# More outputs of the mixing stage in the seven-product form, in another order of units

## The reference, cut to what matters

```python
def conformer_conv(a, conv_w, conv_b, norm_g, norm_b, w_o):
    gl = a[..., :CONV_WIDTH] * jax.nn.sigmoid(a[..., CONV_WIDTH:])
    y = conv_general_dilated(gl, ...31 taps, one filter per channel...) + conv_b
    y = jax.nn.silu(layer_norm(y, norm_g, norm_b))        # over the 1024 channels
    return y @ w_o

def mixer_merge(p, attn, w_attn_o, ..., w_gmlp_o, ..., w_conv_o, w_out):
    a_out = attn @ w_attn_o
    gu = jax.nn.gelu(p[..., GU_OFF:GV_OFF])
    gv = rms_norm(jax.nn.gelu(p[..., GV_OFF:CG_OFF]), gmlp_norm_g)
    g_out = chunk_spatial_gate(gu, gv, gmlp_ws, gmlp_bs) @ w_gmlp_o
    c_out = conformer_conv(p[..., CG_OFF:GATE_OFF], ...)
    gates = jax.nn.sigmoid(p[..., GATE_OFF:])              # three gates of 1024
    return (ga * a_out + gg * g_out + gc * c_out) @ w_out

for l in range(2):                                         # first block, D = 1024
    h = modulate(rms_norm(x, mix_pre_g[l]), sh1, sc1)      # 512 tokens
    p = h @ w_in[l]                                        # 7680 columns
    ...                                                    # the 256 context tokens alike in layer 0
    y = mixer_merge(...)
    x = x + g1 * rms_norm(y, mix_post_g[l])
    x = x + g2 * rms_norm(sq_relu_mlp(h2, w_ff1[l], w_ff2[l]), ffn_post_g[l])
...                                                        # then a second block, not touched
```

## Time and profile before

| | us |
|---|---|
| median of 3 runs | 3997.34 (3994.84 to 3998.64) |
| the profiled execution's own time | 3993.82 |
| its span | 3992.0 |
| PE busy | 3832.3 (96%) |
| DVE busy | 2353.9 (59%) |
| ACT busy | 945.8 (24%) |
| POOL busy | 290.2 (7%) |

### The profile page before, as it was taken

One profiled execution on the slowest core, in us unless ns is written; L12 is line 12 of the kernel. 1 busy time (PEld: TensorE's weight loads), 2 busy tenths in 40 slices (PEclk: granted clock), 3 DMA queues, 4 the chain that ended last, 5 costly groups with the idle time before them and its releaser, 6 DMA issues.

```text
span 3992.0 us, 34044 instructions
## 1 busy us (share of the span) xinstructions
PE 3832.3 (96%) x13274; PEld 2253.6 (56%) x13274; DVE 2353.9 (59%) x3855; ACT 945.8 (24%) x1917; POOL 290.2 (7%) x257
## 2 busy tenths in 40 slices
PE   7999989999999999999999999999999999899999
PEld 3454455555554554554445776646665458657665
DVE  5893548887405456556315599615666456745666
ACT  2103421111403111113125111312111334431111
POOL 1111000122021000000000012210000000000000
PEclk9999999999999999999999999999999999999999
DMA  7652001111212111111210122222222203011221
GB/s 272 213 200 76 6 22 63 43 64 42 95 61 59 63 63 43 63 63 54 75 64 6 44 84 85 85 79 100 85 85 85 81 33 87 9 42 64 85 96 72
DMA packets 126640, 300.51 MB, mean 75 GB/s; under 512 B 5394, under 2 KB 13634, under 8 KB 126480
## 3 DMA queue, kind: packets, MB, share of 16 engines
q1 hardware_dynamic: 108720, 239.73, 16.8%
q0 software_dynamic: 17760, 58.61, 4.4%
HBM read 296.14 MB, written 2.18 MB: 75 GB/s over the span
## 4 chain that ended last, share of the span: by engine, by line
PE 86%; DVE 9%; ACT 2%; DMA 2%; issue 1%; POOL 0%; DVEq 0%; SPq 0%; ACTq 0%
PE psum L447 32%; PE psum L2494 15%; PE psum L2366 14%; PE psum L2418 12%; PE psum L2360 3%; PE psum L1127 2%; PE psum L2463 2%; PE psum L2446 1%; DVE sb_kvt L2797 1%; DMA sb_rc<-in_ada_w 1%; DVE sb_rc L2797 1%; PE psum L1233 1%; DMA sb_ra<-in_ada_w 1%; ACT sb_rb L2047 1%; ACT sb_rc L2047 1%
## 5 line engine op out<-in xcount | busy, mean ns | idle before, releaser
L447 PE MATMUL psum<-sb_ring,sb_rc 128*128 128x512 f32 x868 | 393.3, 594 | 7.5 <-DVE sb_rc L593 7.5
L2887 DVE SCALAR_TENSOR_TENSOR sb_rc<-sb_rc,sb_vec 128x512 f32<-128x512 f32 (+1 forms) x450 | 384.7, 921 | 0.0
L2047 ACT ACTIVATE sb_rc<-psum 128x512 f32<-128x512 f32 (+3 forms) x295 | 147.1, 519 | 991.4 <-DVE sb_ra L609 309.2
L2418 PE MATMUL psum<-sb_ring,sb_ht 128*128 128x512 f32 x832 | 364.5, 596 | 3.5 <-ACT sb_ht L2047 2.8
L447 PE MATMUL psum<-sb_ht,sb_ring 128*128 128x256 f32 (+1 forms) x1152 | 306.7, 416 | 0.0
L447 PEld LDWEIGHTS psum<-sb_ring,sb_rc 128*128 128x128 f32 x868 | 164.8, 190 | 217.0 <-issue 204.7
L2494 PE MATMUL psum<-sb_ht,sb_ring 128*128 128x384 f32 (+1 forms) x960 | 275.5, 435 | 8.0 <-ACT sb_x L2047 7.3
L2047 ACT ACTIVATE sb_rc<-sb_rc 128x512 f32<-128x512 f32 (+3 forms) x248 | 153.1, 682 | 526.2 <-DVE sb_rc L578 526.2
L2366 PE MATMUL psum<-sb_rc,sb_ring 128*128 128x512 f32 (+1 forms) x768 | 276.6, 521 | 0.0
L2418 PEld LDWEIGHTS psum<-sb_ring,sb_ht 128*128 128x128 f32 x832 | 156.8, 191 | 205.7 <-issue 199.2
L447 PE MATMUL psum<-sb_rb,sb_rc 128*128 128x512 f32 x588 | 268.6, 593 | 0.0
(11 more groups left out here) (414 smaller groups left out, 5598.5 us busy)
## 6 DMA issues: line engine op xcount, KB each, us to landing
sb_ring<-in_w_in SPq DMA_DIRECT2D x37, 2048.0 KB, 7.8
sb_ring<-in_w_ff SPq DMA_DIRECT2D x32, 2048.0 KB, 8.0
sb_ring<-in_w_ffn SPq DMA_DIRECT2D x16, 2048.0 KB, 7.8
sb_rc<-in_ada_w POOLq DMA_DIRECT2D x26, 1024.0 KB, 5.7
sb_ra<-in_ada_w POOLq DMA_DIRECT2D x14, 1024.0 KB, 5.8
sb_ring<-in_w_gmlp_o SPq DMA_DIRECT2D x4, 2048.0 KB, 7.6
sb_ring<-in_w_attn_o SPq DMA_DIRECT2D x4, 2048.0 KB, 7.7
sb_ring<-in_w_conv_o SPq DMA_DIRECT2D x4, 2048.0 KB, 7.7
```

The source lines that it names most:

```text
L447: last = pe.matmul(bank(to, width), left[k], right[k], start=k == 0, stop=k == depth - 1)
L2047: return act.activation(out_, in_, f, **kw)
L2418: last = pe.matmul(bank(4 + g % 4, width), lhs[:, k, at:at + P], ring[:, slot, k, 0:width], start=k == 0, stop=k == KT - 1)
L2887: step = stt(out_, in_, vec[:, j, k:k + 1], out_, op0=ALU.mult, op1=ALU.add)
```

## The change

- The gmlp and attention outputs in layer 0 and the convolution's output in both layers become units: 32 in layer 0, 24 in layer 1. In layer 1 the gmlp and attention outputs stay plain, and are issued all 16 together, ahead of the gates (`plain_outs`).
- The right operands of these units need four differences of their own, DVE instructions of 1536 or 1024 elements (`turn_right`), for units 4, 8 and 28 in layer 0 and 28 in layer 1.
- Gate and linear units of the convolution alternate: 0, 2, 1, 3 in place of 0, 1, 2, 3. So two weight blocks are in use by turns, and each becomes free one unit later.
- POOL multiplies and adds a whole unit (1536 or 1024 elements) at a time, while the gate units run. The convolution's part is multiplied and added on DVE (`join`).
- Taps run at 11 or 13 per unit, two of them inside `weight_sums`; 156 beside the plain outputs in layer 1.
- The convolution's sum and mean come at unit 25 in layer 0 (place 25 in the order) and unit 24 in layer 1 (place 16), the variance two places later, and reciprocal, scale and silu three places later.
- The rope table's buffer moves into sb_rc, and x is loaded back earlier.

```diff
-        MIX = 20
-        MIX_BLOCK = (0, 1, 2, 3, 4, 6, 8, 10, 12, 13)
-        MIX_SET = (1, 0, 1, 0, 1, 0, 1, 0, 1, 0, 0, 1, 1, 0, 0, 1, 1, 0, 1, 0)
-        SIGMOIDS, PRODUCTS = (0, 1, 4, 5), (2, 3, 6, 7)
+        SIGMOIDS, PRODUCTS = (0, 1, 12, 13), (2, 3, 14, 15)
+        GATES, OUTS = range(16, 28), (*range(4, 12), *range(28, 32))
+        MIX_UNITS = ((0, 2, 1, 3, *range(4, 12), 12, 14, 13, 15, *range(16, 32)),
+                     (0, 2, 1, 3, 12, 14, 13, 15, *range(16, 32)))
+        MIX = [len(us) for us in MIX_UNITS]
+        MIX_BLOCKS = (tuple(range(16)), (0, 1, 6, 7, 2, 3, 4, 5, *range(8, 16)))
...
+        def mix_freed(l, k):
+
+            b = MIX_BLOCKS[l][k]
+            if l and 2 <= b < 6:
+                return s_bo_ps.at(0, 4 * b - 4)
+            return s_mix_end.at(l, MIX_UNITS[l].index(2 * b + 1) + 1)
...
+        NORM_AT, OUT_TAPS = (25, 24), 156
...
@@ POOL @@
-                    run = 3 * l + b
-                    for j in range(KT):
-                        pool.wait_ge(*s_bo_sb.at(run, j + 1))
-                        o = branch[:, j % 2, 0:n * P]
-                        g = gates[b][:, j, 0:n * P]
-                        if b == 0:
-                            pool.tensor_tensor(g, o, g, ALU.mult).then_inc(s_merged.sem, 1)
-                        else:
-                            ch.link(pool.tensor_tensor(o, o, g, ALU.mult))
-                            pool.tensor_tensor(acc[:, j, 0:n * P], acc[:, j, 0:n * P], o, ALU.add).then_inc(s_merged.sem, 1)
+                for u in range(16, 24):
+                    pool.wait_ge(*s_sigmoid.at(l, u - 11))
+                    p = slice(2 * (u % 4), 2 * (u % 4) + 2)
+                    g = q_cm[:, p, 0:n * P]
+                    if u < 20:
+                        pool.wait_ge(*s_bo_sb.at(0, KT)) if l else None
+                        pool.tensor_tensor(acc[:, p, 0:n * P], acc[:, p, 0:n * P], g, ALU.mult).then_inc(s_merged.sem, 1)
+                    else:
+                        o = u_cm[:, p, 0:n * P]
+                        pool.wait_ge(*s_merged.at(l, u - 19))
+                        ch.link(pool.tensor_tensor(o, o, g, ALU.mult))
+                        pool.tensor_tensor(acc[:, p, 0:n * P], acc[:, p, 0:n * P], o, ALU.add).then_inc(s_merged.sem, 1)
...
@@ DVE @@
+            def weight_sums(l, i, convolve):
...
+                ch.note(tt(s_[:, 0, :, :], a21, a22, ALU.add))
+                done = ch.n
+                convolve(1)
...
+            def turn_right(l, u, m):
+
+                h, right = half_of(l), mix_right(u)
+                before = turned_before(l, u)
+                if m:
+                    dve.wait_ge(*s_mix_t.at(l, before + m))
+                left, minus, to = {
+                    0: (right[:, 0:4, h:2 * h], right[:, 0:4, 0:h], mix_turned(l, u, 0)),
+                    1: (right[:, 4:8, h:2 * h], mix_turned(l, u, 0), mix_turned(l, u, 1)),
+                    2: (right[:, 4:8, h:2 * h], right[:, 0:4, h:2 * h], right[:, 0:4, h:2 * h]),
+                    3: (right[:, 4:8, 0:h], mix_turned(l, u, 1), mix_turned(l, u, 2))}[m]
+                tt(to, left, minus, ALU.subtract).then_inc(s_mix_t.sem, 1)
...
+                ch.link(tt(pair[:, :, 0:n], pair[:, :, 0:n], gate[:, :, 0:n], ALU.mult))
+                tt(total, total, pair[:, :, 0:n], ALU.add).then_inc(s_joined.sem, 1)
...
-                for u in range(16):
-                    first_sum(l, u)
-                    if u - 1 in PRODUCTS:
-                        gated_linear(l, u - 1)
-                    if u >= 4:
-                        convolve(f1)
-                    second_sum(l, u)
-                    if u >= 4:
-                        convolve(f2)
-                    third_sum(l, u)
-                    if u < 8:
-                        weight_sums(l, u + 2)
-                    if u >= 4 and (u < 9 or u % 2 == 0):
-                        convolve(f3)
-                    if u >= 9 and u % 2:
-                        if u < 15:
-                            convolve(f4)
-                        else:
-                            convolve(CONVK * KT)
-                            conv_total(l)
-                        weight_sums(l, u + 1)
-                        convolve(f3)
-                        weight_sums(l, u + 2)
-                        convolve(f3)
-                conv_mean(l)
-                centre(l, range(KT))
-                for step in (first_sum, second_sum, third_sum):
-                    step(l, 16)
-                weight_sums(l, 18)
-                for j in range(1, 4):
-                    add_square(l, j)
-                first_sum(l, 17)
-                for j in range(4, KT):
-                    add_square(l, j)
-                second_sum(l, 17)
-                third_sum(l, 17)
...
+                for i, u in enumerate(MIX_UNITS[l]):
+                    mid = 2 <= i < first
+                    fill = convolve if mid else none
+                    if i == first:
+                        convolve(CONVK * KT)
+                        conv_total(l)
+                        conv_mean(l)
+                        centre(l, range(KT))
+                    if i == first + 3:
+                        dve.wait_ge(*s_std_sb.at(l, 1))
+                        ch.link(dve.reciprocal(kt[:, 1, 0:NT[l] * P], kt[:, 1, 0:NT[l] * P]))
+                        conv_scale(l, range(KT))
+                    if u == 28:
+                        for m in range(4):
+                            dve.wait_ge(*s_conv_cm.at(l, KT if m else 4))
+                            turn_right(l, u, m)
+                    first_sum(l, i)
+                    if l == 0 and u == 7:
+                        dve.wait_ge(*s_att_sb.at(l, OH[l]))
+                        turn_right(l, 8, 0)
+                    if l == 0 and u == 8:
+                        turn_right(l, 8, 3)
+                    if i and MIX_UNITS[l][i - 1] in PRODUCTS and not (l and u == 16):
+                        gated_linear(l, i - 1)
+                        begun[1] += 1
+                    fill(f1)
+                    if i == first + 1:
+                        for j in range(1, 4):
+                            add_square(l, j)
+                    second_sum(l, i)
+                    if l == 0 and u == 7:
+                        turn_right(l, 8, 1)
+                    fill(f2)
+                    third_sum(l, i)
+                    if l == 0 and u == 1:
+                        for m in range(4):
+                            turn_right(l, 4, m)
+                    if l == 0 and u == 7:
+                        turn_right(l, 8, 2)
+                    if i == first + 1:
+                        for j in range(4, KT):
+                            add_square(l, j)
+                    if not (l and u in (13, 15)):
+                        lead(i, fill)
+                    fill(f3)
+                    if l and u == 15:
+                        gated_linear(l, i)
+                        begun[1] += 1
+                        convolve(OUT_TAPS)
+                        lead(i - 1, fill)
+                        lead(i, fill)
+                    if u > 28:
+                        join(l, i - 1)
+                join(l, MIX[l] - 1)
...
@@ PE @@
+                    if l and u == 16:
+                        plain_outs(i - 1)
+                    if i == first:
+                        pe.wait_ge(*s_conv_ready.at(l, KT + 1))
+                        if l:
+                            pe.wait_ge(*s_bo_sb.at(0, 2 * KT))
+                        over_channels(lambda v, a, m: conv_slot(l, KT, v * (TOK + 2 * PAD), m), s_mean_ps)
+                    if i == first + 2:
+                        pe.wait_ge(*s_centred.at(l, KT + 1))
+                        over_channels(lambda v, a, m: u_cm[:, 0, a:a + m], s_var_ps)
```

More of the change, by code:

```diff
@@ L2187, in finished @@
+            def finished(l, i):
+                u = MIX_UNITS[l][i]
                 if u in SIGMOIDS:
-                    act.wait_ge(*s_pads.at(l, 1))
-                    act.wait_ge(*s_mix_last.at(l, u + 1))
-                    for i in range(2):
+                    act.wait_ge(*s_mix_sb.at(l, 3 * i + 3))
+                    act.wait_ge(*s_pads.at(l, 1 + (u >= 12)))
+                    act.wait_ge(*s_mix_last.at(l, i + 1))
+                    for k in range(2):
                         for v, (a, m) in enumerate(streams(l)):
-                            slot = conv_slot(l, 2 * mix_channels(u) + i + 2, PAD + v * (TOK + 2 * PAD), m)
-                            last = fn(slot, mix_pair(u)[:, i, a:a + m], ACT.Sigmoid)
@@ new lines, in finished @@
+                            slot = conv_slot(l, 2 * mix_channels(u) + k + 2, PAD + v * (TOK + 2 * PAD), m)
+                            last = fn(slot, mix_pair(l, u)[:, k, a:a + m], ACT.Sigmoid)
+                    last.then_inc(s_sigmoid.sem, 1)
+                if u in GATES:
+                    act.wait_ge(*s_mix_sb.at(l, 3 * i + 3))
```

(31 more changed lines are left out.)

487 lines of the change are left out of this document (232 added, 255 removed).

## The result

| us | before | after |
|---|---|---|
| median | 3996.09 (4 runs) | 4041.44 (4 runs, 4040.95 to 4041.98) |
| ratio, 95% interval | | 1.0115 (1.0097 to 1.0132) |
| span of the profiled execution | 3992.0 | 4040.2 |
| mixing, layer 0 (first product to first matmul of `token_major`) | 543.30 to 1167.18: 623.9 | 543.60 to 1190.89: 647.3 |
| mixing, layer 1, alike but from its third product | 2222.70 to 2635.23: 412.5 | 2243.31 to 2682.41: 439.1 |

The forecast was 4036 with 4004 to 4062.

The account below looks back on a forecast made before the run. The prediction took PE, busy 96% of the span, as the bound. Matmul work −37.6, old waits −24.5 and new waits +100.6 gave +38.5 us on 3993.82; with 3.5 for the median, 4036, range 4004 to 4062.

Parts of the forecast that it names:

- Matmul work, −37.6: PE's matmul rows removed in both mixing stages: 31.0 us less in layer 0 and 6.6 less in layer 1.
- Mean, variance, unit 28, ends: New PE waits for DVE, with restarts: 13.7, 7.7, 16.0 and 8.7 us in layer 0; 30.5 for layer 1's other places.
- The second wait at unit 28: In layer 0, m2 was to wait 2.0 us more for `turn_right`, behind eight scale instructions on DVE.
- Weight blocks: Blocks free one unit later make sums late: 4 us in layer 0, 14 with restarts in layer 1.
- POOL beside DVE: POOL's merges beside DVE's taps in layer 0 delay PE: 6 us taken, between 0 and 23.
- full price of 23: Layer 0's cost if each POOL merge holds DVE for its length: 23 us in place of 6.
- Restarts: PE's slow starts at the lower clock after new waits in both mixing stages: 16.6 us of the sum.
- The sum: Net change of the profiled execution from work removed, old waits gone and new waits: +38.5 us.
- The prediction's own signs of being wrong: No PE gap at the matmul of ones, gaps over 10 us in units 17 to 24, or PE's busy time not down about 38.
- POOL in full: Rival: POOL holds DVE for 23 us in place of 6, plus 4 in layer 1: 4057; chance 0.18, other additions included.
- Light waits: Rival: restarts cost little, weight blocks are in time, POOL is hidden; half or more gone: about 4015; chance 0.19.
- faster: Rival: mean, variance and scale cost PE only 10.3 us, as the convolution's chain did before: 3988; chance 0.08.

Follow-up runs that it names:

- experiment 12: The kernel of experiment 8 with 16 of the convolution's 31 taps, the other 15 left out: 3961.53 us, ratio 0.9913.
- kernel before cut alike: The kernel before the change with 16 of the convolution's 31 taps, the other 15 left out: 3994.60 us, ratio 1.0.
- experiment 11: The changed kernel with 16 of the convolution's 31 taps, the other 15 left out: 4019.85 us, ratio 1.0062.
- experiment 4: The changed kernel with the convolution's sum over tiles moved behind unit 24's first sum, in both layers: 4029.89 us, ratio 1.0087.
- experiment 7: The changed kernel with POOL's merges on DVE, the convolution's sum early, the variance late and layer 0's scale early: 3990.55 us, ratio 0.9988.
- experiment 5: The changed kernel with the variance's matmul of ones issued behind its unit's third product instead of ahead of the first: 4028.57 us, ratio 1.0084.
- experiment 3: The changed kernel with gate and linear units in the old order (0, 1, 2, 3 and 12, 13, 14, 15): 4027.06 us, ratio 1.0081.
- experiment 1: The changed kernel with POOL's twelve merges per layer cut to 32 columns of each tile, the rest left out: 4021.19 us, ratio 1.0064.
- experiment 8: The kernel of experiment 7 with, in addition, the old order of units and the first three joins ahead of the second sum: 3979.68 us, ratio 0.9963.
- experiment 6: The changed kernel with layer 0's root, reciprocal and scale instructions placed earlier, layer 1 as it was: 4041.88 us, ratio 1.0116.

## Why the prediction was right, and which terms were off

- **Matmul work, −37.6.** It fits, though nothing isolates it: with order and load mended and few taps, experiment 12 is 33.1 us under the kernel before cut alike. In the two traces the mixing stages (from the first product on) are 27.8 and 9.4 us shorter, with 18.4 us of waits in place of 17.6, so waits don't make the gain. PE's 13274 instructions are as before.
- **Mean, variance, unit 28, ends.** Idle by the sum 11.2, 5.2, 13.4 and 5.7 in layer 0; measured 10.94, 5.08, 11.93 (0.73 and 11.20) and 5.35 (0.64 and 4.71). Layer 1: 9.0, 4.0, 3.1 and 4.2; measured 8.61, 3.77, 1.28 and 3.83. Place made the first two: experiment 11 keeps 10.95 with half of the taps, experiments 4 and 7 take it down to 5.79 and 1.58, experiment 5 takes the variance's away. The second wait at unit 28 in layer 0 did not come: m1 ran slowly (5.49), and the turned operand was there in time; where m1 took 4.28 (experiment 7), PE waited 0.88 for it.
- **Weight blocks.** 4 in layer 0 (1.52 and 1.61), 10 in layer 1 (4.03, 3.49, 0.26), and 2.3 behind the plain outputs (3.38). Experiment 3 shows the cause: all of these are gone there but the last (3.56 in place of 3.38). DVE's wait for the block in layer 0, answering to the 10.31 of the earlier trace rows, was

```profile
826.92 0.69 DVE L2937 TENSOR_TENSOR sb_kvt<-sb_ring 128x512 f32<-128x512 f32 x1 [11.07 <-DMA sb_ring<-in_w_in]
```

- **POOL beside DVE, taken at 6 from a range of 0 to 23: mis-sized.** PE idled 15.5 for it, and with its restarts it cost 20.4 (experiment 1), near the upper end. The choice leaned on one row of 22 taps in a stream, which POOL did not break into the earlier trace rows. But taps now alternate with weight sums, and each unit's first merge got in at the same spot, between L2942 and the tap behind it, in seven units of seven; why there and not between taps is not shown. What the prediction quoted of the Trainium skill (SBUF — State Buffer, section "SBUF: two separate sides"), a lock for whole instructions, is what the trace shows: 3.2 us lost beside an instruction of 3.49. The prediction's full price of 23 was the better one for layer 0; in layer 1 (4) it cost nothing: two merges held taps for 1.3 and 1.7 us without a product waiting, the others came when the taps had run out at 2498.
- **Restarts.** Inside both stages 25.5 us in place of 16.6: busy time 595.3 and 410.4, where the plain arithmetic (623.9 − 9.9 − 1.8 − 31.0, and 412.5 − 6.9 − 6.6) leaves 581.2 and 399.0. At the mean PE started with

```profile
1028.04:1030.04 2.00, 2.00 (x3) 0.97 (x4) 0.00 (x0) 0.00 (x0) 0.00 (x0) 0.50 0.00 0
1030.04:1032.04 2.00, 2.00 (x5) 1.22 (x4) 1.02 (x2) 0.00 (x0) 0.00 (x0) 0.50 0.00 0
```

  (a window's start and end, length, PE, PEld, DVE, ACT and POOL busy, granted clock, DMA): the lower level for these 4 us, and 0.61 in the 2 us behind them. In the kernel before, the 2 us behind those of the earlier trace rows had 0.65. The 25.5 hold what POOL's waits cost in restarts.
- **The sum.** Forecast +38.5, measured +48.2 between the profiled spans: layer 0 +23.4, layer 1 +26.6, the first matmuls behind the stages −2.7 (65.03 to 63.59 and 51.13 to 49.91), the rest +0.9. New idle was 80.6 for 78.1; the surplus of POOL (+9.5) and of the restarts (+8.9) met 7.0 of waits that were smaller. So the sum was 9.7 short, and the forecast of the median only 5.4: it had added 3.5, by which the median stood above the profiled execution before, and after the change the median lies 0.5 below it. That part is luck.
- **The prediction's own signs of being wrong.** PE had its gap at the matmul of ones. The two others came. The gaps of units 17 to 23 sum to 15.5 us, over the 10 that were to put POOL in the first place: it is the term that was sized wrong. And PE's busy time fell by 14.3 and not by about 38. That speaks less against the matmul work than against the sign: rows at the lower clock count as busy, so of 37.6 the restarts inside the stages put back 25.5, while 1.8 of old ones went there and 2.7 behind them: 16.6 less by this sum.
- **What the prediction did not see.** That it matters when DVE's long work can start. It had put DVE at 16.5 of 18.06 us a unit and looked only for waits in the units themselves. In the order that was forecast this cost nothing at the mean, where DVE idled 7.1 us in unit 24; in the old order it costs 11 to 12 us there (experiments 3, 8 and 12). Its rival "POOL in full" at 4057 lies 15.6 above the measured time: layer 1's 4 did not come, and layer 0's idle was 15.5 in place of 23; what took up the rest is not shown. "Light waits" and "faster" fall.

## What to carry to other kernels

Where plain work is turned into a cheaper form that another engine has to serve, add up that engine's load from the point where its long work can start to the point where the engines meet, and not per unit. If it is full all that way, a wait removed ahead of the meeting point comes back at it (experiment 3); if it has time to spare there, only the order of its work counts. A reduction that a later matmul needs belongs ahead of the next short sum on its engine, and the matmul a product or two late: each such place was worth 5 to 9 us here for a few moved lines (experiments 4 and 5, from the wait ahead of it to the stage's end). And wide POOL instructions beside a full DVE cost DVE about their length, more than doing the work there (3.2 against 1.75 us); beside a DVE with time to spare, in layer 1, they cost nothing.

## What the runs showed of the hardware beyond that

- In the changed kernel a POOL tensor_tensor of 1536 elements took 3.43 to 4.06 us, DVE's of the same shape 1.75.
- PE's restarts were not alike after like waits. After 1.9 to 2.7 us idle a close took 2.85 in most places, but 4.16 to 4.54 in four (experiments 3, 5, 6 and 7); after 4.38 idle it always ran slowly, and took from 4.25 (experiment 3) to 5.49 (experiment 6). So gaps of the same length cost up to 1.7 us apart, and a comparison of a few us between two kernels needs more than one trace of each.
